# Norm steps, state space, head loads and paired scores moved in one two-layer kernel on a Trainium2 core

## The chip, the cores and the metric

The kernel runs on one core of one Trainium2 chip. A core has TensorE (PE in the profile, which multiplies and transposes), VectorE (DVE), ScalarE (ACT) and GpSimd (POOL), each with its own instructions in a fixed order, and SyncE (SP), whose queue issues nearly all loads and stores. Engines wait for each other only where a semaphore is named. The metric is the device time of one execution, in microseconds. The kernel before took 3650.94 us, the median of three runs (3649.84 to 3656.97).

## The reference

Two layers of a language model on 1024 tokens of width 1024, in float32. The first layer puts 16 more tokens ahead, so it works on 1040.

```python
# layer 1, mixer
h = rmsnorm(x, g_pre); u,q,k,v,o,gi,gf,ga,gb = split(h @ w_in)
y_a = gelu(s5_ssm(u, ...)); y_a = y_a * sigmoid(y_a @ w_glu)        # state space
hb  = mlstm_chunkwise(q, k, v, log_i, log_f)                        # gated matrix memory
merged = sigmoid(ga) * (y_a @ w_a) + sigmoid(gb) * (norm(hb) * sigmoid(o) @ w_b)
x = x + rmsnorm(merged @ w_out, g_post)
# layer 1, channel mixer
h = rmsnorm(x, g_pre)
x = x + rmsnorm((gelu(conv(h @ w_gate)) * (h @ w_up)) @ w_down, g_post)
# layer 2
proj = rmsnorm(x) @ w_in_2
y_rwkv = rwkv7_mixer(proj[..., :RWKV])     # 8 heads of 64, a recurrence over time
y_attn = dilated_attention(proj[..., RWKV:])   # 8 heads of 64, causal, three patterns in one softmax
x = x + concat(y_rwkv, y_attn) @ w_out_2
x = x + (silu(conv(rmsnorm(x) @ gate)) * (rmsnorm(x) @ val)) @ w_down_2
return rmsnorm(x)
```

A softmaxed score of the attention is q times k over the 64 numbers of one head.

## The kernel before

Activations lie with their 1024 features on 8 x 128 partitions and the tokens along the free axis. A product in float32 is made of three matmuls: each operand is split into a rounded part and a rest (hi and lo), and hi x hi, lo x hi and hi x lo are added up in one bank. `dense` does a tile of 128 output features: for each chunk of tokens (264, 264 and 512 in layer 1, 512 and 512 in layer 2) 8 x 3 matmuls into one bank. Weights are loaded by SP four tiles ahead and split two tiles ahead, hi by ACT and lo by DVE (`w_hi`, `w_lo`).

The order of every engine is written out by hand. A `Lane` stands for one engine. The stages follow one another: norm, first projections (in1: u, v, o, q, k and NG of the 16 g tiles), the state space's output gate (glu), the other g tiles (in2), the merge and w_out (out1), the channel mixer (ffn), the second layer's projections (in3), its heads, and again out and ffn. What runs beside a stage is a generator in `bg`, whose pieces end in `yield`. `tick` advances it by `rate` steps at the end of each chunk: RS = 3 beside in1 for the state space, RM = 4 beside in2 for the mLSTM, 1 beside glu for the gate transposes (`mgates`). With `fine` set, `slots(1)` after each three matmuls on PE, and `slots(8)` at each chunk on ACT and DVE, advance it by a step each; this is how norms are worked into the tiles of the next stage. PRE is the number of empty steps before the state space's first matmul, which wants `ssm_Cop`, made by POOL from DVE's `ssm_W`.

A joined norm (`joined_pe`, `joined_act`, `joined_dve`, `joined_pool`) ends a layer's part: a sum of squares over features by a matmul with ones (the root "sum"), then for eight row blocks m: DVE scales the block (`SCALAR_TENSOR_TENSOR HB<-HB,vecs,over1l..`), POOL adds the residual, ACT squares it, and DVE adds the square to the last ones; the root "sum2" by PE; then eight blocks y are scaled and split into hi and lo for the next stage. It is done for each half of the tokens: in the profile these are the tiles `extra` (first half) and `over1lB` and `over1lA` (second half). `plain_*` and `final_*` are norms with one root, in layer 2.

in3 has 52 tiles. Its results are stored to DRAM (`rkv`, `attn`), since the heads need the memory. The heads are three streams braided step by step: rwkv for two groups of heads, the second LAG = 20 steps behind, and attention. The attention for a pair of heads j goes over 16 units u, that is the row block i = u // 2 and the head h = u % 2; scores, mask and maximum by DVE, exponential by ACT, transposes by PE, copy by ACT, values by PE, copy by ACT. Its banks are a ring of four (`atb`), taken in turn: `take` waits until the old contents of a bank were read. The query is kept as `a_qz`, 128 partitions by two copies, with zeros in the other head's 64 rows, so that one 128-row matmul gives the score of one head.

## Time and profile before

| what | value |
|---|---|
| median of three runs | 3650.94 us |
| the profiled execution's own time | 3654.43 us |
| its span in the profile | 3652.6 us |
| TensorE busy | 3327.2 us, 91% |
| VectorE busy | 1757.6 us, 48% |
| ScalarE busy | 1187.3 us, 33% |
| GpSimd busy | 236.9 us, 6% |
| mean granted clock of TensorE | 0.954 |

A busy share is an average over stages that are limited by different things. Where TensorE is idle, the page and the trace name the engine and the tile whose semaphore released it; that name is inferred from the last event. A matmul of 128 rows by 512 columns comes every 0.22 us at the full clock. "PEclk" is the granted clock as a share of full speed: 0.50 is 1.2 GHz, 1.00 is 2.4 GHz.

### The profile page before, as it was taken

The page shows a single profiled execution, that of the slowest core. Times are in us where ns is not written, and L with a number is a line of the kernel's source. Part 1 is how long each engine was busy: PE and PEld are TensorE (multiplying, and loading weights), DVE is VectorE, ACT ScalarE, POOL GpSimd, SP SyncE. Part 2 cuts the span into 40 slices and gives each one's busy share as a digit, 9 for nine tenths or more (in the row PEclk, how much of TensorE's full clock was granted, in tenths as well). Part 3 has the DMA queues.
Part 4 walks back from the last instruction along what each step waited for, and adds up shares of the span by engine and source line. Part 5 has one row for each costly group of instructions (what it writes and reads, how often), then busy time and mean ns, then how long its engine had stood idle before and what let it go on. Part 6 is the DMA issues. An engine that isn't in the chain of part 4 may idle for free. (4 is left out here: it accounts for less than half of the span.)

```text
span 3652.6 us, 55140 instructions
## 1 busy us (share of the span) xinstructions
PE 3327.2 (91%) x23686; PEld 2767.0 (76%) x23686; DVE 1757.6 (48%) x2928; ACT 1187.3 (33%) x2054; POOL 236.9 (6%) x212
## 2 busy tenths in 40 slices
PE   5699989998979999999889978988977999999998
PEld 4588877787858888888667857776756778888887
DVE  6544533336475243435664435454554664333355
ACT  4112335542353221213433233434322432212133
POOL 1211000002130000000120000000001000000000
PEclk9899999999989999999999989998989999999999
DMA  2111112213423111123433330001001322111123
GB/s 98 41 53 47 65 62 84 80 55 125 142 75 120 59 46 53 42 61 109 135 135 128 130 108 19 10 28 36 2 19 39 107 89 71 49 47 52 47 93 110
DMA packets 86834, 262.28 MB, mean 72 GB/s; under 512 B 10272, under 2 KB 10400, under 8 KB 86464
## 3 DMA queue, kind: packets, MB, share of 16 engines
q1 hardware_dynamic: 76576, 224.07, 18.7%
q0 software_dynamic: 5120, 16.86, 1.3%
q10 hardware_dynamic: 4896, 17.84, 1.2%
q8 instruction: 187, 3.06, 0.4%
q14 instruction: 55, 0.45, 0.0%
HBM read 216.51 MB, written 42.21 MB: 71 GB/s over the span
## 5 line engine op out<-in xcount | busy, mean ns | idle before, releaser
L157 DVE TENSOR_TENSOR w_lo<-w_raw,w_hi 128x1024 fp32r<-128x1024 f32 (+3 forms) x353 | 398.3, 1130 | 440.5 <-ACT w_hi L154 438.4
L123 PE MATMUL ps<-XHA,w_hi 128*128 128x264 f32 (+3 forms) x1456 | 475.0, 326 | 20.6 <-DVE XLA L157 6.6
L123 PE MATMUL ps<-XLA,w_hi 128*128 128x264 f32 (+3 forms) x1456 | 462.9, 318 | 0.0
L123 PE MATMUL ps<-XHA,w_lo 128*128 128x264 f32 (+3 forms) x1456 | 461.2, 317 | 0.0
L154 ACT ACTIVATE w_hi<-w_raw 128x1024 fp32r<-128x1024 f32 (+3 forms) x353 | 339.9, 963 | 347.7 <-PE ps L123 285.0
L123 PE MATMUL ps<-XHB,w_hi 128*128 128x512 f32 x920 | 369.5, 402 | 9.2 <-POOL XLB L157 6.2
L123 PE MATMUL ps<-XLB,w_hi 128*128 128x512 f32 x920 | 360.6, 392 | 0.0
L123 PE MATMUL ps<-XHB,w_lo 128*128 128x512 f32 x920 | 360.2, 392 | 0.0
L123 PEld LDWEIGHTS ps<-XHA,w_hi 128*128 128x128 f32 x1456 | 281.6, 193 | 53.9 <-issue 25.0
L123 PEld LDWEIGHTS ps<-XLA,w_hi 128*128 128x128 f32 x1456 | 281.6, 193 | 22.6 <-issue 4.6
L123 PEld LDWEIGHTS ps<-XHA,w_lo 128*128 128x128 f32 x1456 | 281.7, 193 | 16.6
L123 PEld LDWEIGHTS ps<-XHB,w_hi 128*128 128x128 f32 x920 | 174.1, 189 | 52.4 <-issue 11.6
L123 PEld LDWEIGHTS ps<-XLB,w_hi 128*128 128x128 f32 x920 | 174.1, 189 | 38.2 <-issue 3.6
L123 PEld LDWEIGHTS ps<-XHB,w_lo 128*128 128x128 f32 x920 | 173.9, 189 | 37.0
L157 DVE TENSOR_TENSOR HB<-HB,ps 128x512 f32<-128x512 f32 (+1 forms) x136 | 88.4, 656 | 218.2 <-PE ps L123 215.7
L123 PE MATMUL ps<-X2HA,w_hi 128*128 128x512 f32 x416 | 163.6, 393 | 11.0 <-DVE X2LA L157 5.2
L123 PE MATMUL ps<-X2HB,w_hi 128*128 128x512 f32 x416 | 162.7, 391 | 1.4 <-issue 1.4
L123 PE MATMUL ps<-X2LA,w_hi 128*128 128x512 f32 x416 | 162.8, 391 | 0.0
L123 PE MATMUL ps<-X2HA,w_lo 128*128 128x512 f32 x416 | 162.7, 391 | 0.0
L123 PE MATMUL ps<-X2HB,w_lo 128*128 128x512 f32 x416 | 161.9, 389 | 0.0
L123 PE MATMUL ps<-X2LB,w_hi 128*128 128x512 f32 x416 | 161.8, 389 | 0.0
L164 DVE TENSOR_SCALAR C<-G,vecs 128x512 f32<-128x512 f32 x88 | 49.8, 566 | 224.7 <-ACT G L154 224.7
(446 smaller groups left out, 6344.1 us busy)
## 6 DMA issues: line engine op xcount, KB each, us to landing
w_raw<-in_f_gate SPq DMA_DIRECT2D x66, 512.0 KB, 3.3
w_raw<-in_f_up SPq DMA_DIRECT2D x66, 512.0 KB, 3.3
w_raw<-in_w_out SPq DMA_DIRECT2D x32, 512.0 KB, 3.4
w_raw<-in_f_down SPq DMA_DIRECT2D x48, 320.0 KB, 2.9
w_raw<-in_f_down SPq DMA_DIRECT2D x32, 384.0 KB, 3.1
w_raw<-in_w_rkv SPq DMA_DIRECT2D x24, 512.0 KB, 3.4
w_raw<-in_w_attn SPq DMA_DIRECT2D x24, 512.0 KB, 3.4
w_raw<-in_w_qkvo SPq DMA_DIRECT2D x16, 512.0 KB, 3.3
```

Of the source, the lines that this page charges most:

```text
L123: return Issued(e.matmul(out, a, b, start=start, stop=stop))
L154: return Issued(self.eng and self.eng.activation(out, src, ACT.Copy))
L157: return Issued(self.eng and self.eng.tensor_tensor(out, a, b, op))
L164: return Issued(self.eng.tensor_scalar(out, a, s1, s2, op0, op1))
```

## The change

Five things are changed together.

1. Two more g tiles go from in2 to in1 (NG 2 to 4), the state space begins 24 steps later (PRE 18 to 42), and the mLSTM runs at five steps per chunk (RM 4 to 5) beside the 12 g tiles that are left.
2. The gate transposes pause 10 steps where they paused 3, and are not drained after glu: they are done after the first chunk of in2.
3. Chunks up to 300 columns wide give a turn after every second k only (`turns_at`). The joined norm's pieces stand three turns apart (its blocks m) and two (its blocks y), and PE's roots later; the plain norms likewise.
4. Loads and constants of the heads are issued beside in3: at the tile `EARLY` the lora weights, the mask and the first rwkv inputs (`rwkv_load`), at `LATER` the first attention inputs (`attention_load`). The heads' memory is laid out anew, so that these land on tiles nobody uses then.
5. The query is one tile without zeros (`a_q`). The scores of two heads are two 64-row matmuls, on the upper and the lower half of the partitions, one behind the other in PE's order. PE's steps of a pair are now: transpose of the unit before, values of the one before that, scores of both.

Removed and added lines of the core:

```diff
-LAG, K0, RS, RM, NG, PRE, MID, POST, HN, Q1, Q2, Q3, Q4, Q5 = 20, 1, 3, 4, 2, 18, 18, 8, 8, 1, 1, 1, 1, 1
+LAG, K0, RS, RM, NG, PRE, MID, POST, HN, Q1, Q2, Q3, Q4, Q5 = 20, 1, 3, 5, 4, 42, 18, 8, 8, 1, 1, 1, 1, 1
...
-            if k < kt - 1:
+            if k < kt - 1 and turns_at(cn, k):
                 P.slots(1)
+def turns_at(cn, k):
+    return cn > 300 or k % 2
...
 def joined_pe(P, K, N, c):
-    yield from pause(4)
+    yield from pause(7)
     root_pe(P, K, N, c, "sum", ("acc", c, 7))
-    yield from pause(8)
-    yield from pause(8)
-    yield from pause(8)
+    yield from pause(37)
     root_pe(P, K, N, c, "sum2", ("acc2", c, 7))
-    yield from pause(16)
+    yield from pause(18)
...
 def joined_dve(V, K, N, c, gain, gnext, free):
-    yield from pause(8)
+    yield from pause(11)
     free(V)
     root_dve(V, N, c, "sum")
-    yield from pause(4)
...
         if m >= 2:
             add(m - 2)
-        yield
+        yield from pause(3)
+    yield
     add(6)
+    yield from pause(3)
     add(7)
-    yield from pause(12)
+    yield from pause(7)
     root_dve(V, N, c, "sum2")
...
+EARLY, LATER = (1, "rkv", 6), (1, "aqkv", 8)
...
+        if t == EARLY:
+            n3_over(D, K)
+            D.dma(K.wl[:, :], K.I["lora_wa"]).then_inc(K.lora, by=16)
+            D.dma(K.gl[:, :], K.I["lora_g"]).then_inc(K.lora, by=16)
+            D.dma(K.amask[:, :], K.I["a_mask"]).then_inc(K.a_mask, by=16)
+            for g in range(2):
+                ...
+                rwkv_load(D, K, g, 0)
+        if t == LATER:
+            ...
+            attention_load(D, K, 0)
...
+def rwkv_load(D, K, g, u):
+    T, (j, hf) = K.rw[g], halves(g)[u]
+    for n in range(3):
+        D.dma(T.in3[:, n, :], K.rkv[4 * n + j][:, 512 * hf:512 * hf + 512]).then_inc(T.ld, ("in", u), by=16)
...
+def attention_load(D, K, j):
+    S = K.at
+    D.dma(K.aq[:, :], K.attn[j]).then_inc(K.a_ld, by=16)
+    D.dma(K.ak[:, :], K.attn[4 + j]).then_inc(K.a_ld, by=16)
+    if j:
+        D.wait_ge(S.pe, ("t", j - 1, 15))
+    D.dma(K.aA[(18 * j) % 2][:, :], K.attn[8 + j]).then_inc(K.a_ld, ("in", j), by=16)
...
-                    P.mm(b[:, 0:cn], K.qz[:, h, 128 * i:128 * i + 128], K.ak[:, c0:c0 + cn], True, True).then_inc(
-                        S.pe, ("s", j, u, c0))
+        def scores(u):
+            i = u // 2
+            chunks = [(c0, min(512, 128 * (i + 1) - c0)) for c0 in range(0, 128 * (i + 1), 512)]
+            banks = [[ps.take(P, ("s", j, u + h, c0)) for c0, _ in chunks] for h in range(2)]
+            for n, (c0, cn) in enumerate(chunks):
+                for h in range(2):
+                    P.mm(banks[h][n][:, 0:cn], K.aq[heads(h), 128 * i:128 * i + 128], K.ak[heads(h), c0:c0 + cn], True,
+                         True).then_inc(S.pe, ("s", j, u + h, c0))
         for u in range(18):
+            if u % 2 and u < 16:
                 yield
             if 1 <= u < 17:
+                turn(u - 1)
             if u >= 2:
+                values(u - 2)
+            if u % 2 == 0 and u < 16:
+                scores(u)
+                yield
             yield
```

What moves, on PE in the first projections, where `ssm_Cop,ssm_Bn` is the state space's first matmul and the `XHA`, `XLA` rows are the projection's. Before:

```order
L123 MATMUL ps<-XHA,w_hi 128x264
L123 MATMUL ps<-XLA,w_hi 128x264
L123 MATMUL ps<-XHA,w_lo 128x264
L122 MATMUL ps<-ssm_Cop,ssm_Bn 32x256 x8
L123 MATMUL ps<-XHA,w_hi 128x264
L123 MATMUL ps<-XLA,w_hi 128x264
L123 MATMUL ps<-XHA,w_lo 128x264
```

It stands there after the first chunk of the fourth tile. Now:

```order
L123 MATMUL ps<-XHB,w_hi 128x512
L123 MATMUL ps<-XLB,w_hi 128x512
L123 MATMUL ps<-XHB,w_lo 128x512
L122 MATMUL ps<-ssm_Cop,ssm_Bn 32x256 x8
L123 MATMUL ps<-XHA,w_hi 128x264
L123 MATMUL ps<-XLA,w_hi 128x264
```

It moved behind the last chunk of a tile, eight chunks or 192 matmuls on.

On DVE in the first joined norm of a layer, beside the last tiles of w_out: `HB<-HB,vecs,over1lB` is the scaling of a block, `extra<-extra` and `extra<-extra,over1lB` the adds of squares, `over1lB<-over1lB,extra` and `w_lo` the tiles' own work. Before:

```order
L167 SCALAR_TENSOR_TENSOR HB<-HB,vecs,over1lB 128x514 x4
L157 TENSOR_TENSOR extra<-extra,over1lB 128x514
L157 TENSOR_TENSOR over1lB<-over1lB,extra 128x512
L157 TENSOR_TENSOR w_lo<-w_raw,w_hi 128x1024
L167 SCALAR_TENSOR_TENSOR HB<-HB,vecs,over1lB 128x514
L157 TENSOR_TENSOR extra<-extra 128x514
L167 SCALAR_TENSOR_TENSOR HB<-HB,vecs,over1lB 128x514
L157 TENSOR_TENSOR extra<-extra,over1lB 128x514
L167 SCALAR_TENSOR_TENSOR HB<-HB,vecs,over1lB 128x514
L157 TENSOR_TENSOR extra<-extra 128x514
```

Now:

```order
L167 SCALAR_TENSOR_TENSOR HB<-HB,vecs,over1lB 128x514 x2
L157 TENSOR_TENSOR over1lB<-over1lB,extra 128x512
L157 TENSOR_TENSOR w_lo<-w_raw,w_hi 128x1024
L167 SCALAR_TENSOR_TENSOR HB<-HB,vecs,over1lB 128x514 x2
L157 TENSOR_TENSOR extra<-extra,over1lB 128x514
L167 SCALAR_TENSOR_TENSOR HB<-HB,vecs,over1lB 128x514
L157 TENSOR_TENSOR extra<-extra 128x514
L157 TENSOR_TENSOR over1lB<-over1lB,extra 128x512
L157 TENSOR_TENSOR w_lo<-w_raw,w_hi 128x1024
L167 SCALAR_TENSOR_TENSOR HB<-HB,vecs,over1lB 128x514
```

The tiles' work now stands after every second or third block instead of once.

On PE in the heads, in the attention's fourth and fifth row blocks: `a_k,a_qz` or `a_k,a_q` are scores, `cst,a_A` transposes, `a_VT,a_PT` values, the others rwkv's. Before:

```order
L123 MATMUL ps<-a_k,a_qz 128x384
L123 MATMUL ps<-r_t,cst 128x512
L126 MATMUL ps<-cst,a_A 128x128 x3
L123 MATMUL ps<-a_VT,a_PT 128x64 x2
L123 MATMUL ps<-r_Xa,r_GB 64x64 x16
L123 MATMUL ps<-a_k,a_qz 128x512
```

Now:

```order
L126 MATMUL ps<-cst,a_A 128x128 x3
L123 MATMUL ps<-a_VT,a_PT 128x64 x2
L123 MATMUL ps<-r_Xa,r_GB 64x64 x16
L126 MATMUL ps<-cst,a_A 128x128 x3
L123 MATMUL ps<-a_VT,a_PT 128x64 x3
L123 MATMUL ps<-a_k,a_q 128x512 x2
```

Two scores stand together, behind two turns of transposes and values.

## Rows read from the trace of the kernel before

**Rows 1.** The page, part 1: busy us (share) xinstructions
```profile
PE 3327.2 (91%) x23686; PEld 2767.0 (76%) x23686; DVE 1757.6 (48%) x2928; ACT 1187.3 (33%) x2054; POOL 236.9 (6%) x212
```

**Rows 2.** Waits of PE: engine, tile, line, releaser: total us, times, longest
```profile
PE ps L123 <- DVE r_in L157: 31.1, 25, 3.6
PE ps L123 <- DVE extra L157: 26.0, 2, 14.4
PE ps L122 <- POOL ssm_Cop L163: 25.4, 1, 25.4
...
PE ps L123 <- DVE over1lB L157: 19.4, 2, 19.0
...
PE ps L123 <- DVE over1lA L157: 15.7, 1, 15.7
...
PE ps L126 <- ACT HB L136: 11.9, 1, 11.9
PE ps L123 <- DMA r_gl<-in_lora_g: 11.9, 1, 11.9
...
PE ps L126 <- DMA a_A<-attn: 6.9, 1, 6.9
```

**Rows 3.** Timeline, first projections: start, us, engine, line, operation, [idle <-releaser]
```profile
124.70 1.22 DVE L157 TENSOR_TENSOR w_lo<-w_raw,w_hi 128x1024 fp32r<-128x1024 f32 x1
124.88 7.28 POOL L163 TENSOR_SCALAR ssm_Cop<-ssm_W,cst 128x1152 f32<-128x1152 f32 x2 [8.93 <-DVE ssm_W L157]
...
132.21 1.93 PE L122 MATMUL ps<-ssm_Cop,ssm_Bn 128*32 128x256 f32 x16 [25.44 <-POOL ssm_Cop L163]
```

**Rows 4.** Timeline of ACT, output gate of the state space
```profile
524.62 1.07 ACT L136 ACTIVATE HB<-HB 4x1040 f32<-4x1040 f32 x1 [10.31 <-DVE HB L157]
...
527.00 0.88 ACT L136 ACTIVATE glu_s<-ps 128x264 f32<-128x264 f32 x2
```

**Rows 5.** Windows: us; busy PE, PEld, DVE, ACT, POOL; clock, DMA share, GB/s
```profile
545.00:845.00 300.00, 272.81 (x1617) 231.42 (x1616) 104.76 (x200) 150.43 (x257) 14.19 (x15) 0.95 0.21 74
1013.50:1016.00 2.50, 2.50 (x7) 1.95 (x6) 0.87 (x1) 2.42 (x5) 0.00 (x0) 0.50 0.23 39
2200.00:2650.00 450.00, 404.01 (x6240) 324.22 (x6239) 238.51 (x480) 163.62 (x372) 15.72 (x10) 0.93 0.06 19
```

**Rows 6.** Timeline of DVE, first norm of the group
```profile
989.56 4.62 DVE L167 SCALAR_TENSOR_TENSOR HB<-HB,vecs,over1lB 128x514 f32<-128x514 f32 x4
...
1011.25 0.70 DVE L157 TENSOR_TENSOR extra<-extra,over1lB 128x514 f32<-128x514 f32 x1
```

**Rows 7.** Timeline of DVE, second norm of the group
```profile
1068.61 0.74 DVE L167 SCALAR_TENSOR_TENSOR HB<-HB,vecs,over1lB 128x512 f32<-128x512 f32 x1
1069.45 1.78 DVE L157 TENSOR_TENSOR over1lB<-over1lB 128x512 f32<-128x512 f32 x1
```

**Rows 8.** Timeline of PE, second channel mixer
```profile
2940.26 0.47 PE L123 MATMUL ps<-X2HA,w_hi 128*128 128x512 f32 x1 [3.46 <-issue]
```

**Rows 9.** Timeline of all engines, start of the heads
```profile
2142.61 0.56 SPq L192 DMA_DIRECT2D r_wl<-in_lora_wa  x1
...
2151.09 0.69 DVE L157 TENSOR_TENSOR r_t<-r_t 128x512 f32<-128x512 f32 x1
...
2155.24 1.97 PE L126 MATMUL ps<-cst,a_A 128*128 128x128 f32 x8 [6.86 <-DMA a_A<-attn]
...
2157.43 1.92 PE L123 MATMUL ps<-r_t,cst 128*128 128x512 f32 x2
```

**Rows 10.** The tile a_qz on PE: duration ns min/median/max, first, last, forms
```profile
L123 PE MATMUL ps<-a_k,a_qz x192: 272/592/1220, 2157.0 to 2626.5; 128*128 128x512 f32 x96, 128*128 128x128 f32 x32, 128*128 128x256 f32 x32, 128*128 128x384 f32 x32
```

**Rows 11.** Timeline of PE and ACT in the heads
```profile
2192.33 1.13 PE L123 MATMUL ps<-r_WA,r_wl 32*128 32x512 f32 x4
...
2241.19 0.22 ACT L154 ACTIVATE HB<-ps 128x64 f32<-128x64 f32 x1
...
2309.57 2.04 PE L123 MATMUL ps<-r_WA,r_wl 32*128 32x512 f32 x4
```

224 lines of the change are left out of this document (117 added, 107 removed).

## The prediction

> **What bounds the kernel now.** The page's first part comes first: TensorE (PE) is busy 3327.2 of 3652.6 us and VectorE 1757.6 [rows 1], so the multiplies' own time is the floor and a change can win by closing PE's idle stretches or by making its instructions overlap. The list of waits by engine then names the idle ones [rows 2]: 25.4 us for one POOL result, 26.0, 19.4 and 15.7 us for four sums of norms made by VectorE, 11.9 us for an exponential of the gates, 11.9 and 6.9 us for two loads at the start of the heads. Each of these belongs to an edit of the change. The timelines around them [rows 3, 4, 6, 7, 9] say what the released work would do next; the windows and the score rows [rows 5, 10, 11] are for the two edits that change how densely PE is fed. The profiled execution took 3654.43 us, 1.8 beyond its span and 3.5 above the median of 3650.94; the sum is made against 3654.4, and 3.5 is taken off at the end. What this kernel's measurement can tell from no change is about 0.2%, 7.3 us.
>
> **1. State space 24 steps later.** PE stops inside the fourth projection tile and resumes 25.44 us later, at 132.21, because the state space's first matmul stands there in its order and wants Cop, which POOL finishes at 132.2 [rows 3]. VectorE's and POOL's preparation keep their places. With 24 steps at three per chunk the matmul stands eight chunks on, so tile four (begun at 101.9, 11.5 us of matmuls) ends near 113.6 and tile five near 125.1. Tile six's lo weights are split from 124.70 to 125.92, since VectorE waits for POOL's Bop before: 0.8 us is late next. Cop is ready long before PE gets to it. After the stall PE's 264-wide matmuls run 0.22 us apart instead of 0.12, at the lower of the two clocks (granted 0.50 where the same happens at 1013.5 [rows 5]), about 1.5 us. Sum: -25.4 - 1.5 + 0.8 = **-26** (-22 to -28). The two g tiles moved from the second to the first projection stage cost the same matmuls in either place: 0.
>
> **2. Gate transposes after the first chunk of the next stage.** They wait 11.88 us for the exponential, which itself waits for VectorE's scans and ends at 525.7 [rows 2, 4]. But the sigmoids of the output gate stand behind that exponential on ScalarE and start at 527.00 [rows 4], and PE has four banks to fill before it needs one of them. So PE stops a few chunks later for nearly as long: about 3 us go, and the 2 us of the first wait for m_D behind it: **-5** (-2 to -12, the whole wait).
>
> **3. The mLSTM five steps to a chunk instead of four.** Same steps beside 12 tiles, not 14. PE is idle 300.00 - 272.81 = 27.2 us in its stretch [rows 5], mostly on short chains of other engines of 0.7 to 3.1 us at a time. These chains' lengths stay, the cover shrinks to four fifths, so I let the idle grow by a quarter: **+7** (-3 to +27, the idle doubled).
>
> **4. Norms spread.** Four times PE reaches the second root sum before VectorE has it: 11.6, 19.0, 14.4 and 15.7 us (the extra and over1l rows [rows 2]). In PE's order that sum now stands 44 rows later (116 rows of 258 columns for the second), 10 us of matmuls (13.7). But VectorE's order now has the work of the tiles between the norm's steps, and that work delays the sum. For the first: first scaling at 989.56, last square added at 1012.0 [rows 6], 22.4 us of which 3.5 are idle. It starts 1.1 us later, and where one weight split and one add of the tiles' stood between the steps there are now four and five: 3 x 1.23 + 4 x 0.69 = 6.5 us more, and they take up the idle 3.5: 989.6 + 1.1 + 22.4 - 3.5 + 6.5 = 1016.1, against PE there at 1010.4: a stall of 5.7, 5.9 less. The same sum for the others, whose first scalings start at 1047.37, 1721.69 and 1825.33 and whose stalls begin at 1053.9, 1730.3 and 1834.9: 1047.4 + 3.4 + 25.4 - 3.9 + 5.1 = 1077.4 against 1067.6 (9.2 less); 1721.7 + 1.1 + 22.9 - 1.8 + 5.7 = 1749.6 against 1740.3 (5.1 less); 1825.3 + 1.1 + 25.2 - 3.5 + 5.4 = 1853.5 against 1844.9 (7.1 less). The last addend is two more splits and four or five of the tiles' other operations, 0.55 to 0.77 us each, counted in the two orders. Sum **-27**. Bounds: 0 if ScalarE's waits come in again at each step, -65 if all four vanish (60.7 and 1.2 each of low clock). The price per step carries this: VectorE needs 0.74 for a scaling and 1.78 for the add [rows 7], 2.5 together, while the last add, with POOL done, takes 0.70 [rows 6]. The adds are long beside POOL's residual add, which starts when the scaling ends, and spreading doesn't change that.
> The Trainium skill, "SBUF — State Buffer", in its summary of rules for kernel authors, says that when VectorE reads two operands from SBUF while GpSimd reads there, the later one waits for the other. The rows agree (1.78 against 0.70). By that rule a spread norm is still blocked for all of POOL's time if VectorE has tile work then, which is my sum; only where the spread leaves VectorE idle beside POOL would the adds fall to 0.70, which is rival A.
> Beside the last output projection and the second channel mixer the simple norms are spread too; PE's waits for it at 2892.11, 2940.26 (3.46 us [rows 8]) and 2947.7 are 6.5 us: **-5.5** (0 to -7).
>
> **5. Heads' loads made earlier.** PE has 11.9 us of idle until the lora weights' landing, then 6.9 until the attention's v [rows 2]: SP issues the first of them at 2142.61, after the last spill has landed, and v lands by 2155.24 [rows 9]. Now all but the last tiles' spills come ahead of them. What stays is the last projection's spill, so PE starts at about 2142.5, 3.8 earlier. After the scores its next matmul (at 2157.43) needs r_t, which VectorE has at 2151.8 [rows 9]; 3.8 earlier that is 2148.0, and v no longer stands before it, so 2157.4 - 2148.0 = 9.4 is gained: **-9.4** (-6 to -12). Twelve loads now go out among the weights' of the projection's last tiles; one that made a weight 4 us late would cost 4, and the lower bound leaves it in. POOL's memsets go from a time when nobody waits: 0.
>
> **6. Two heads' scores by row groups.** Now a score multiplies 128 rows, half of them zeros: 192 records [rows 10], 36,864 columns in all. After, two heads' scores stand in two halves of 64 rows, next to each other in PE's order. What rows show of such a pair: of the lora pairs (two row groups, 512 columns each), one at 2192.33 takes 1.13 us for both and one at 2309.57 2.04 us [rows 11]; in the first the two overlap, in the second a bank's wait stood between them. So a 512-wide pair is worth 0.91 us, and 36 of them (36,864 / 1024) 32.8 us of PE. Against it: from the fifth row block a pair takes all four banks and waits for ScalarE's copy of the values just computed (0.22 us [rows 11], 0.5 with the way there): 16 pairs, 8 us. PE is busy 404.01 of 450 us there [rows 5], the rest is waited for VectorE's chains, so I let 0.8 of 24.8 reach the span: **-20** (+5: they run one after the other, and the wait is paid; -35: all).
> The Trainium skill speaks on both sides: "TensorEngine Tiling (Array Packing)", key properties, lets different tiles load and multiply in parallel, and says that changing the tiling mode drains TensorE. The fast lora pair agrees with the first. No row here separates the second; the pairs need fewer such changes than single scores, not more, so it is no part of the sum.
>
> **Sum.** -26 - 5 + 7 - 27 - 5.5 - 9.4 - 20 = -85.9: 3654.4 - 85.9 = 3568.5, less 3.5 of the median: **3565**.
>
> **Rivals.**
> A, the norms' stalls vanish: VectorE is only 48% busy over the kernel and idles 3.5 us for ScalarE in the first of these norms, and such idle time would take the tiles' work. Against it the in-order sum above. 38 more: 3527.
> B, heads and mLSTM give less: row groups side by side need both weights in place and no bank wait between; the slow lora pair speaks for it, and the mLSTM's idle grows by 20 rather than 7. 20 + 13: 3598; with the norms giving only half, 3612.
> C, slower than before: the take of four banks ties the heads' three braided streams to each other. ScalarE's copies stand behind its waits for rwkv's steps, those behind PE's, and PE stands at the scores. VectorE's r_in is waited for 25 times already, up to 3.6 us each [rows 2]. The scores' 20 us would be gone and 16 waits of 0.5 us (8 in all, in the sum already) would be longer ones; the whole comes to 3658 and is slower from (3658 - 3565 - 20 + 8) / 16 = 5.1 us a wait on. At 6 us: 3565 + 20 - 8 + 96 = 3673. Against it, ScalarE's copy starts within 0.1 us of the values' end in the row at 2241.19 [rows 11].
> D, the scores run as before in time, and all else holds: 3565 + 20 + 5 = 3590; the pairs' records would not start together.
>
> **How the numbers follow.** Forecast 0.52, A 0.15, B 0.16, D 0.14, C 0.03. The likeliest is 3565, its own range 3545 to 3585. The range reaches to A and past D and B, without B's worst: 3525 to 3606. Faster by over 7.3 us holds A, B, D and the forecast but for their ends: 0.95; within it 0.02, from those ends; slower 0.03, C.
>
> **What would show it.** The profile after: no wait of PE for Cop, and the clock full from 102 on; the four waits for extra and over1l at 6, 10, 9 and 9 us (all gone: A; as before: step 4 is wrong); the waits for r_gl and v gone; PE's busy time 25 to 35 us less, the score records of two heads starting within 0.01 us of each other and their mean near today's; the stretch of in2 with about 34 us idle. The prediction is wrong if the sum2 waits keep their length, if the heads' stretch (671 us from 2147 to 2818) is not shorter by 15, or if a new wait for ScalarE's HB stands before the scores.

## The result, and the profile after

The changed kernel takes 3630.81 us, the median of four runs (3630.16 to 3631.42), beside 3652.1 for the kernel before in its four runs of the comparison: a ratio of 0.994 (95%: 0.9923 to 0.9957). It is faster, by 21 us, and not by the 86 that were forecast; 3565 and the range up to 3606 were both missed. The profiled execution took 3631.2 us with a span of 3629.4, 23.2 less than the 3652.6 before.

Part 1 of the page after, which answers to [rows 1]:

```profile
PE 3319.5 (91%) x23686; PEld 2772.5 (76%) x23686; DVE 1741.7 (48%) x2928; ACT 1181.3 (33%) x2050; POOL 242.1 (7%) x210
```

PE has as many matmuls as before and is busy 7.7 us less, where 25 to 35 were forecast. The place of the difference is found by cutting both spans at the same matmuls. The two g tiles (22.8 us) that went from in2 to in1 are taken out of both.

| stretch | before | after | change, without the moved tiles | forecast |
|---|---|---|---|---|
| first projections | 455.72 | 456.80 | -21.7 | -26 |
| output gate | 39.33 | 37.17 | -2.2 | -5 |
| in2 beside the mLSTM | 291.03 | 284.42 | +16.2 | +7 |
| merge to first w_down, first pair of joined norms | 366.16 | 358.84 | -7.3 | -15.1 |
| around the second pair | 235.91 | 229.67 | -6.2 | -12.2 |
| heads, from in3's last matmul to w_out's first | 687.46 | 687.96 | +0.5 | -29.4 |
| w_out and start of the second channel mixer | 230.11 | 228.09 | -2.0 | -5.5 |

The rest (1,347 us) differs by 0.4. Nearly half of what is missing lies in one row, the heads.

The waits of PE after (engine, tile, line, releaser: total us, times, longest), the answer to [rows 2]:

```profile
PE ps L123 <- DVE r_in L157: 37.9, 27, 3.6
...
PE ps L123 <- DVE m_SS L167: 21.1, 13, 3.8
...
PE ps L123 <- DVE r_t L157: 20.2, 21, 3.9
PE ps L123 <- DVE r_S L157: 18.6, 27, 3.8
PE ps L123 <- DVE extra L157: 13.7, 2, 9.0
PE ps L123 <- ACT r_BK L154: 13.5, 5, 4.1
PE ps L123 <- DVE ssm_Dop L177: 13.1, 3, 7.8
...
PE ps L123 <- ACT glu_s L136: 12.1, 1, 12.1
PE ps L123 <- DVE over1lB L157: 8.9, 1, 8.9
PE ps L123 <- DVE over1lA L157: 8.0, 1, 8.0
...
PE ps L123 <- ACT HB L154: 6.8, 17, 0.6
```

Gone are the rows for POOL's Cop, for the two loads at the start of the heads, and for the exponential. The norms' rows fell from 61.1 to 30.6 us. But four kinds are new or longer: the gates' sigmoid `glu_s` (12.1, in the place of the exponential's 11.9), `m_SS` of the mLSTM (8.2 before), rwkv's four tiles `r_in`, `r_t`, `r_S` and `r_BK` (31.1, 13.9, 13.4 and 9.1 before), and 17 short ones for `HB`, the copy of the attention's values.

The timeline of PE and DVE at the places of steps 1, 2 and 4 (start, us, engine, line, operation, [idle before <- releaser]):

```profile
124.38 2.35 DVE L157 TENSOR_TENSOR w_lo<-w_raw,w_hi 128x1024 fp32r<-128x1024 f32 x2
...
528.25 0.79 PE L123 MATMUL ps<-glu_h,w_hi 128*128 128x512 f32 x1 [12.06 <-ACT glu_s L136]
...
1008.30 2.08 PE L123 MATMUL ps<-extra,cst 128*128 128x258 f32 x4 [4.72 <-DVE extra L157]
...
1028.22 0.36 PE L123 MATMUL ps<-XHA,w_hi 128*128 128x258 f32 x1 [1.15 <-POOL XLA L157]
...
1073.80 2.07 PE L123 MATMUL ps<-over1lB,cst 128*128 128x512 f32 x2 [8.93 <-DVE over1lB L157]
...
1103.74 0.36 PE L123 MATMUL ps<-XHA,w_hi 128*128 128x258 f32 x1 [2.22 <-issue]
...
1724.66 0.47 PE L123 MATMUL ps<-XHB,w_hi 128*128 128x512 f32 x1 [2.16 <-issue]
...
1737.36 2.07 PE L123 MATMUL ps<-extra,cst 128*128 128x512 f32 x2 [9.01 <-DVE extra L157]
...
1772.74 0.50 PE L123 MATMUL ps<-PH1B,w_hi 128*128 128x512 f32 x1 [3.16 <-DVE PL1B L157]
...
1840.59 2.07 PE L123 MATMUL ps<-over1lA,cst 128*128 128x512 f32 x2 [8.04 <-DVE over1lA L157]
```

Each norm still has its root wait (4.7, 8.9, 9.0, 8.0), and beside it stand waits that were not there: the first matmuls on the blocks that the spread norm has just made, and two at 1103.74 and 1724.66 for which the profile names no releaser. PE stops at 528.25 for the sigmoids as long as it stopped for the exponential.

The start of the heads and a pair of scores on PE, for [rows 9] and [rows 11], and the tile of the scores, for [rows 10] (durations in ns, lowest/median/highest):

```profile
2121.26 2.07 PE L123 MATMUL ps<-r_WA,r_wl 32*128 32x512 f32 x4 [8.33 <-issue]
...
2126.51 2.04 PE L123 MATMUL ps<-r_t,cst 128*128 128x512 f32 x2 [0.55 <-DVE r_t L157]
...
2280.41 1.13 PE L123 MATMUL ps<-a_k,a_q 64*128 64x512 f32 x4
```

```profile
L123 PE MATMUL ps<-a_k,a_q x192: 269/589/1218, 2125.2 to 2601.4; 64*128 64x512 f32 x96, 64*128 64x128 f32 x32, 64*128 64x256 f32 x32, 64*128 64x384 f32 x32
```

Both parts of the change to the heads do what they say. From in3's end to the matmul of `r_t` it is 14.4 us where it was 23.9. One pair of scores of 512 columns takes 1.13 us for both, the records of the two start 7 ns apart (35 ns in the second chunk of a wide row block), and PE is occupied by scores 42.8 us in all where it was 82.6 (the union of the 192 records). And yet the stretch is as long as before. Where the 39.8 us went, the windows of that stretch tell (us; busy PE, PEld, DVE, ACT, POOL with counts; mean granted clock, DMA share, GB/s). Before:

```profile
2133.58:2821.04 687.46, 568.54 (x9154) 453.21 (x9154) 345.72 (x670) 225.24 (x486) 28.75 (x21) 0.90 0.08 23
```

After:

```profile
2112.07:2800.03 687.96, 551.56 (x9154) 453.55 (x9154) 341.93 (x669) 224.99 (x484) 25.97 (x17) 0.87 0.05 18
```

PE is busy 17 us less, not 40, its clock fell from 0.90 to 0.87, and it is idle 136.4 us instead of 118.9. To put a price on the clock, each stretch below is cut into windows of 2 us, and PE's busy time in each is parted into busy x granted clock ("work", what it would take at 2.4 GHz) and the rest ("lost to the clock", what the same matmuls took longer at 1.2 GHz). Stretch = work + lost + idle. Each row is one execution, the profiled one. All kernels are in the table, since the experiments are read by it.

| heads of | stretch | work | lost to the clock | idle |
|---|---|---|---|---|
| before | 687.5 | 519.7 | 48.8 | 118.9 |
| after | 688.0 | 484.2 | 67.3 | 136.4 |
| e1 single scores, old order | 684.5 | 522.0 | 57.4 | 105.1 |
| e2 new order, full rows | 701.0 | 512.9 | 58.1 | 130.0 |
| e3 rate by chunk | 687.8 | 484.2 | 66.9 | 136.7 |
| e4 blocks y closer | 676.0 | 485.7 | 54.3 | 136.0 |
| e5 gates spread | 688.0 | 484.3 | 67.2 | 136.5 |
| e6 pairs inside the old order | 677.4 | 509.9 | 56.5 | 111.0 |
| e7 eight idle matmuls ahead | 681.1 | 492.0 | 58.8 | 130.2 |
| e8 root later, y closer | 676.0 | 485.8 | 54.3 | 136.0 |
| e9 all together | 675.9 | 517.1 | 52.9 | 105.9 |
| e10 after + 40 idle of 256 columns | 684.3 | 508.8 | 55.3 | 120.2 |
| e11 e9 with the norms of after | 677.3 | 516.5 | 55.8 | 105.0 |
| e12 e1 + eight idle matmuls ahead | 687.8 | 529.4 | 56.2 | 102.3 |
| e13 after + 40 idle of 512 columns | 698.0 | 526.3 | 53.8 | 117.9 |
| e14 e9 + 40 idle of 256 columns | 689.5 | 540.6 | 56.4 | 92.5 |
| e15 before + 40 idle of 256 columns | 690.5 | 542.8 | 39.2 | 108.5 |

From before to after the work fell by 35.5 us; 17.5 of it came back as idle time and 18.5 as time lost to the lower clock. The two are not equally firm. after, e3, e4, e5 and e8 have the same instructions in the heads: their work and idle times agree to 1.6 and 0.7 us, while 66.9 to 67.3 us are lost to the clock in three of them and 54.3 in the other two.

### The profile page after: what moved, and what is told of

Same layout as the page of the kernel before. It is cut to its first block, busy times and chain, and to the rows that moved or that the text cites. A ratio compares the mean times of both kernels' runs of the same rounds, so it can differ in the third digit from the quotient of the medians.

```text
span 3629.4 us, 55150 instructions
## 1 busy us (share of the span) xinstructions
PE 3319.5 (91%) x23686; PEld 2772.5 (76%) x23686; DVE 1741.7 (48%) x2928; ACT 1181.3 (33%) x2050; POOL 242.1 (7%) x210
## 4 chain that ended last, share of the span: by engine, by line
PE 76%; DVE 14%; ACT 6%; issue 3%; DMA 1%; POOL 1%; ACTq 0%; DVEq 0%; SPq 0%; POOLq 0%
PE ps L123 73%; PE ps L122 2%; PE ps L126 2%; DVE w_lo L157 1%; ACT L136 1%; ACT w_hi L154 1%; DVE r_t L157 1%; DVE HB L167 1%; DVE m_S L167 1%; DVE r_in L157 1%; ACT m_D L136 1%; DVE HB L157 1%; DVE r_Xa L157 1%; DVE r_t L167 0%; ACT r_t L136 0%
```

## The experiments

Each ratio is against the kernel before on the same chip. "Idle matmuls" are matmuls whose result nobody reads.

Most kernels here share all stages but one with after, so the traces also tell how far a stage moves when nothing in it is changed:

| stretch | kernels with after's instructions there | us |
|---|---|---|
| first projections | all but before and e15 | 454.7 to 456.9 |
| output gate | all of those but e5, e9, e11, e14 | 37.2 to 38.4 |
| in2 | after, e1, e2, e4, e6, e7, e8, e10, e12, e13 | 282.5 to 287.9 |
| merge to first w_down | all but before, e15, e4, e8, e9, e14 | 355.7 to 358.9 |
| around the second pair | the same | 229.4 to 229.7 |
| heads | after, e3, e4, e5, e8 | 676.0 to 688.0 |
| w_out and start of the channel mixer | all but before, e15, e4, e8 | 226.4 to 228.1 |

A difference inside such a range is not shown to be the edit's.

### Which part of the change to the scores costs what

The first kernel gives each score its own step again, in the old order, but with 64 rows:

```diff
-            if u % 2 == 0 and u < 16:
-                scores(u)
-                yield
...
+            if u < 16:
...
+                    b = ps.take(P, ("s", j, u, c0))
+                    P.mm(b[:, 0:cn], K.aq[heads(h), 128 * i:128 * i + 128], K.ak[heads(h), c0:c0 + cn], True, True).then_inc(
```

> The changed kernel with the attention's PE and ScalarE steps in their order of before: each head's scores alone, in their own step, as 64-row matmuls on the unpadded query. The early loads and all else stay. Read is the heads' stretch, from the end of the last projection matmul to the first matmul of the output projection: 687.5 us before, 688.0 us in the changed kernel. Theory one (the order of pairs costs what their overlap gives): the stretch falls to 678, the early loads' 9 us being the only gain left, and the kernel runs at 3621 instead of 3631. Theory two (the early loads gain nothing, since another chain is as late as they were): 687, and 3630. TensorE's busy time of the score records goes back from 43 us to about 80 in both.

The second keeps the pairs' order and lets both matmuls use all 128 rows, so that they cannot run side by side (each score is then the sum over both heads, not what the reference computes):

```diff
-                    P.mm(banks[h][n][:, 0:cn], K.aq[heads(h), 128 * i:128 * i + 128], K.ak[heads(h), c0:c0 + cn], True,
+                    P.mm(banks[h][n][:, 0:cn], K.aq[:, 128 * i:128 * i + 128], K.ak[:, c0:c0 + cn], True,
```

> The changed kernel with its order of pairs, but each score multiplies all 128 rows (query and key of both heads), so that the two of a pair can't overlap: the scores are those of the two heads added up, which is not what the reference computes. TensorE gets about 40 us of matmuls back, in the same places. Theory one (TensorE's time counts in the heads, and the pairs' order costs about as much): the stretch grows from 688 by 20 to 35 us, to 708 to 723. Theory two (the heads are bound by chains over VectorE and ScalarE, and time taken from TensorE turns into its waiting): it grows by less than 8, to at most 696, and TensorE's waits for r_in, r_t and r_S shrink by about 30 us.

Measured: e1 3627.27 us (0.9935, 0.9921 to 0.995), e2 3645.63 (0.9989, 0.998 to 0.9999). Windows of the heads, e1:

```profile
2111.67:2796.22 684.55, 579.40 (x9154) 457.68 (x9154) 346.04 (x669) 223.62 (x484) 25.88 (x17) 0.89 0.05 18
```

and e2:

```profile
2107.05:2808.09 701.04, 571.01 (x9155) 461.14 (x9154) 342.70 (x669) 225.08 (x484) 25.98 (x17) 0.89 0.05 17
```

Both stretches lie between the two theories of their kernel: 684.5 between 678 and 687, 701.0 between 696 and 708. e2's profiled execution is the fastest of its ten, 3638.38 us, so its 701.0 is rather short than typical.

The three kernels part the edit in two. The order alone (e1 to e2) adds 24.9 us of idle time and makes the stretch 16.5 longer. It takes 9.1 us of work away: two scores that stand one behind the other overlap in part, and the records of all scores occupy PE 73.1 us in e2 and 84.6 in e1. Full rows or half rows make no difference to a single score (median record 592 and 589 ns). Running side by side (e2 to after) takes 28.7 us of work away, of which 13 reach the end: 6.4 return as idle and 9.2 to the clock. So in work and idle time together the order costs 15.8 us and the overlap gains 22.3, and the pairs of after are 6.5 us ahead of e1. That the stretch of after is 3.4 us longer than e1's all the same is 9.9 us more lost to the clock, and this part is not the edit's for certain: e4 and e8 have the same pairs and take 676.0. The waits of PE in the heads show where the order costs. e1:

```profile
PE ps L123 <- DVE r_in L157: 29.5, 25, 3.6
...
PE ps L123 <- DVE r_t L157: 14.3, 16, 3.6
PE ps L123 <- DVE r_S L157: 13.3, 20, 3.8
PE ps L123 <- ACT r_BK L154: 9.1, 4, 4.1
```

e2:

```profile
PE ps L123 <- DVE r_in L157: 33.2, 26, 3.6
PE ps L123 <- DVE r_t L157: 18.7, 21, 3.8
PE ps L123 <- DVE r_S L157: 18.0, 26, 3.8
PE ps L123 <- ACT r_BK L154: 13.6, 5, 4.1
...
PE ps L123 <- ACT HB L154: 6.9, 17, 0.6
```

The banks (`HB`, 6.9) are the smaller part and are what the prediction had priced at 8. The larger are rwkv's own chains, 17.3 us longer over four rows. In the old order each of the braid's steps had some attention work, which covered a chain. With pairs, by the `yield`s of the new code, two of every four steps have none.

The sixth kernel puts that to use: the old order, and a pair only for the first four row blocks, where it needs two banks:

```diff
+                both = (0, 1) if i < 4 else (h,)
+                if h in both[0:1]:
+                    for c0 in range(0, 128 * (i + 1), 512):
+                        bs = [ps.take(P, ("s", j, 2 * i + g, c0)) for g in both]
+                        for g, b in zip(both, bs):
+                            P.mm(b[:, 0:cn], K.aq[heads(g), 128 * i:128 * i + 128], K.ak[heads(g), c0:c0 + cn], True,
...
```

> The changed kernel with the attention in its order of before, each turn of transposes and values in the step after a score, but with the scores of both heads side by side, as two row groups, in the first four row blocks, where a pair needs two of the four banks; row blocks five to eight have single scores. 10 of 36 parts of the columns are paired. Read is the heads' stretch: 687.5 before, 688.0 in the changed kernel, 684.6 with single scores in the old order, 701.0 with the new order and no overlap. Theory one (the order of pairs leaves two of four steps without attention work, which costs about 16 us, and overlap is worth 13 to 25 for all columns): 677 to 682. Theory two (overlap gains nothing here since TensorE waits anyway): 684 to 686. If the early loads and single scores were already at the bound of VectorE's chains, theory two.

3617.51 us (0.9901, 0.9884 to 0.9917), 13.3 below after. The stretch is 677.4, inside the first theory's 677 to 682: idle stays near e1's (111.0) and 12 us of work are gone. So it is better than e1. Against after it proves less. Work and idle time together are 620.9 us in e6 and 620.6 in after, and the 10.6 us between the stretches are all clock; e4 and e8, with every score in a pair and the order of after, are at 676.0. Which of the two orders is the better one in the heads stays open.

### The lower clock in the heads

One pair of kernels was not made for this and says the most. e4 (below) and after have the same instructions in the heads. Their first 40 us, after:

```profile
2121.26:2161.26 40.00, 33.38 (x276) 23.64 (x276) 17.70 (x36) 18.32 (x46) 2.94 (x2) 0.60 0.00 1
```

and e4:

```profile
2118.00:2158.00 40.00, 32.66 (x318) 22.73 (x320) 18.93 (x41) 19.73 (x48) 2.94 (x2) 0.75 0.01 1
```

The granted clock is 0.60 in the one and 0.75 in the other, and 276 against 318 matmuls are through. Over the whole stretch the same instructions take 688.0 and 676.0 us, with work and idle time equal to 1.5 us and 13.0 less lost to the clock. In both PE stood idle for the 8.3 us ahead of the first of these matmuls. It is not chance from one kernel to the next: the lower clock sets in 5.8 to 6.1 us ahead of the first matmul of the heads and lasts 37.5 us in after, e3 and e5, and it sets in 4.1 us ahead and lasts 20.5 in e4 and e8. It doesn't go by the time at which the heads begin either: in3 ends at 2108.8 in e4 and e8 and at 2100.4, 2107.2 and 2112.1 in e3, e5 and after.

Can matmuls that nobody needs buy the clock back? First, eight of them ahead of the heads, in the time of that wait:

```diff
 def heads_pe(P, K):
+    b = K.fg.take(P, "warm")
+    for _ in range(8):
+        P.mm(b[:, 0:512], K.ident, K.cst[:, 0:512], True, True)
```

> The changed kernel with eight matmuls of a 128x128 by 128x512 constant into a free bank put on TensorE between the last projection and the heads, where it is idle for 9.2 us. They compute nothing that is used. In the changed kernel the granted clock is 0.50 in the first 32 us of the heads; two executions with the same instructions in the heads took 678.8 and 666.9 us there, with 173 and 145 us at the lower clock. Theory one (the idle stretch ahead is what leaves the clock low, and the clock costs): less than 16 of the first 32 us are at 0.50, and the heads' 678.8 us fall by 4 to 12. Theory two (the start is a chain of ScalarE and VectorE and the clock falls again at once): within 3 us, and 2 us more where the matmuls last longer than the idle time.

3622.24 us (0.9917, 0.9902 to 0.9931): 681.1 instead of 688.0, and 8.5 us less lost. Less was lost here. The same eight put into e1:

> Single 64-row scores in the old order (its heads' stretch was 684.6, 3 us less than before, where the early loads should give 9.4) with the eight idle matmuls ahead of the heads. Theory one (the early loads' other 6 us were lost to the clock, which was at 0.50 for 31.6 us of the first 40 where it was 24.3 before): 677 to 680, and at most 25 us of the first 40 at the lower clock. Theory two (another chain is late there, whatever the clock): 683 to 686.

3629.45 us (0.9943, 0.9928 to 0.9958), 2 above e1 instead of below it, though the two intervals overlap. The stretch of 687.8 is longer than either theory had it. Its first 40 us:

```profile
2120.50:2160.50 40.00, 33.69 (x221) 22.53 (x222) 16.23 (x32) 16.27 (x41) 2.95 (x2) 0.56 0.00 1
```

The clock is 0.56 there, and 0.60 in e1 without the matmuls ahead. What they did is to put the fall off: the lower clock sets in 0.8 us behind the first matmul of the heads in e7 and 0.9 behind it in e12, where it came 5.8 and 5.9 ahead of it in after and e1. But it comes all the same, for 23.9 of the next 27 us in e7 and 41.0 of the next 44 in e12. My explanation, that the idle time ahead of the heads brings the clock down and filling it keeps it up, is not borne out; e7's 7 us are of the size of what e4 got by no edit of the heads.

Then 40 idle matmuls in the middle of rwkv's steps, each ahead of a wait for VectorE:

```diff
+            b = D.ps.take(P, (("Y", lv), u))
+            P.mm(b[:, 0:256], K.ident, K.cst[:, 0:256], True, True)
-            products(("Y", lv), lambda h, c: [(x.GB[heads(h), c, 0, :], x.X[heads(h), block(c)])])
+            products(("Y", lv), lambda h, c: [(x.GB[heads(h), c, 0, :], x.X[heads(h), block(c)])], b)
```

> The changed kernel with one more matmul on TensorE ahead of each wait of rwkv for the next power (40 times in the heads, a constant of 128x128 by 256 columns, about 0.43 us each, 17 us in all, into the bank that is overwritten next; nothing of it is used). The heads' stretch is 688.0 us with 173 us of it at the lower clock. Theory one (idle time of TensorE lowers its clock and that is why time taken from it doesn't reach the end): at most 160 us at the lower clock, and the stretch between 680 and 692 in spite of 17 us more work. Theory two (TensorE's time counts by itself, and the clock has little to do with it): 696 to 705, with the time at the lower clock within 10 us of 173.

3626.0 us (0.9934, 0.9917 to 0.995), with a stretch of 684.3: 24.6 us more work, 16.2 less idle, 12.0 less lost. With 512 columns instead of 256:

> The changed kernel with the 40 idle matmuls of 512 columns instead of 256, 34 us of added work for TensorE at the full clock instead of 17. Without them the heads' stretch was 688.0 us with 173 us at the lower clock, with the smaller ones 684.3 and 146. Theory one (the clock pays for added work up to a point, then TensorE's time counts): 125 to 145 us at the lower clock and a stretch of 686 to 698, longer than with 17 us of work but by less than the added 17. Theory two (the 3.7 us gained with the smaller ones were chance in where the clock fell): 700 to 710.

3639.07 us (0.9972, 0.9961 to 0.9983), stretch 698.0, the long end of the first theory: 42.1 more work against 18.5 of idle and 13.5 of the clock. In the kernel before, with 256 columns:

> The kernel before with the same 40 idle matmuls of 256 columns. Its heads' stretch is 687.5 us with 132 us at the lower clock, so the clock has less to give back, while there is more of TensorE's own work (scores 40 us longer). Theory one (the price of added work depends on how much of the stretch is at the lower clock): it grows by 2 to 12 us, clearly more than in the changed kernel, where 17 us of work took 3.7 away. Theory two (added work ahead of these waits is free in any case, since the waits are longer than it): within 2 of 687.5.

3651.92 us (1.0007, 0.9997 to 1.0016), stretch 690.5, 3.0 longer: 23.1 more work, 10.4 less idle, 9.6 less lost, as the first theory had it. So most of such work is paid for by idle time and clock that it takes away, but not all; only in after, the kernel with most idle time and most low clock, is the sum a gain. It is 4 us, work and idle time together are 8.4 us more, and the 12.0 of the clock are less than the 13.0 that e4 had without any edit of the heads; so this gain is not shown to be the idle matmuls'.

### The mLSTM's rate

Chunks of in2 are 264, 264 and 512 columns wide, and each gets five steps. Here they get 4, 4 and 7, the same 15 for a tile:

```diff
-LAG, K0, RS, RM, NG, PRE, MID, POST, HN, Q1, Q2, Q3, Q4, Q5 = 20, 1, 3, 5, 4, 42, 18, 8, 8, 1, 1, 1, 1, 1
+LAG, K0, RS, RM, NG, PRE, MID, POST, HN, Q1, Q2, Q3, Q4, Q5 = 20, 1, 3, (4, 4, 7), 4, 42, 18, 8, 8, 1, 1, 1, 1, 1
-    def tick(self):
-        self.step(self.rate)
+    def tick(self, c=0):
+        self.step(self.rate[c] if isinstance(self.rate, tuple) else self.rate)
```

> The changed kernel with the mLSTM's 15 steps to a tile dealt out 4, 4 and 7 to the chunks of 264, 264 and 512 columns instead of 5, 5 and 5. Read is the stretch from the end of the output gate's projection to the merge: 291.0 before with 14 tiles, 284.4 in the changed kernel with 12 (two tiles are 22.8 us, so 16.2 more than its matmuls). Theory one (the short chunks are too short to cover five steps): 284.4 falls by 5 to 10. Theory two (it is the density over the whole stage that is short, not its unevenness): within 3 of 284.4, since the wide chunk then carries seven steps with waits of their own.

3618.89 us (0.9914, 0.9899 to 0.9928), 11.9 below after. Windows of in2, before:

```profile
539.94:830.97 291.03, 266.63 (x1584) 226.26 (x1585) 93.25 (x194) 142.86 (x237) 1.66 (x8) 0.96 0.22 77
```

after:

```profile
538.60:823.02 284.42, 245.78 (x1458) 205.66 (x1459) 90.23 (x192) 131.43 (x227) 1.66 (x8) 0.96 0.20 72
```

and with 4, 4 and 7:

```profile
538.99:813.82 274.83, 240.65 (x1459) 201.47 (x1459) 90.28 (x192) 131.62 (x227) 1.67 (x8) 0.97 0.21 74
```

Idle time is 24.4, 38.6 and 34.2 us. The stretch with even dealing is 274.8 = 291.0 - 22.8 + 6.6: the 7 forecast for a denser mLSTM is what it costs if the steps are dealt by width. Of the other 9.6, 4.5 are idle time, from five steps beside a 264-wide chunk, whose matmuls are too short to cover them: in2 idles 37.2 to 40.0 us in the ten kernels with five steps and 33.2 to 34.2 in the four with 4, 4 and 7 (e3, e9, e11, e14). The other 5.1 are in the busy time of the same matmuls, at 0.96 of the clock instead of 0.97; 7.3 to 13.5 us are lost to the clock in the ten and 4.9 to 7.8 in the four, so how much of this is the dealing's is not settled.

### The joined norms

Blocks y are made one turn apart instead of two, so that the next stage's matmuls find them:

```diff
 def normed_dve(V, K, N, c, gnext, name):
-        yield from pause(2)
+        yield
...
     rest(7)
+    yield from pause(8)
```

> The changed kernel with the last part of each norm (the eight blocks y) one turn apart again, as before, the blocks m still three apart. Read are the stretches around the norms: from the merge's end to the first down projection 263.0 before and 255.4 in the changed kernel, and around the second norm pair 235.9 and 229.7. Theory one (the waits that came up anew, about 6 us at 1028 to 1040, 4 us at 1098 to 1108 and 7 us at 1724 to 1773 in the changed kernel, are for the y blocks that now come two turns apart): they go, and the stretches fall by 6 to 10 and by 3 to 7; in all 3618 instead of 3631. Theory two (they come from the second root standing 15 turns later): within 2 of the changed kernel.

3622.67 us (0.9925, 0.991 to 0.994), 8 below after. But the heads, in which nothing is changed, are 12.0 us shorter for their clock (above), and the span only 10.3 (3619.1 beside 3629.4), so the rest is longer by 1.7. By places: -1.5 around the first pair and -0.2 around the second, both inside the ranges of kernels without this edit, and +4.5 behind w_out of the second layer, far outside (232.6). That is the second theory's case. PE's timeline has other waits in the place of those that went:

```profile
1056.08 0.77 PE L123 MATMUL ps<-XHA,w_hi 128*128 128x512 f32 x1 [3.20 <-DVE w_lo L157]
...
1068.75 2.07 PE L123 MATMUL ps<-over1lB,cst 128*128 128x512 f32 x2 [7.51 <-DVE over1lB L157]
...
1761.01 0.77 PE L123 MATMUL ps<-XHB,w_hi 128*128 128x512 f32 x1 [5.15 <-issue]
...
2912.32 0.77 PE L123 MATMUL ps<-X2HA,w_hi 128*128 128x512 f32 x1 [5.05 <-issue]
```

The one at 1056.08 waits for a tile's weights: VectorE makes the blocks in a row and splits the weights behind them. For the last two the profile names no releaser. Next, e4 with the second root eight turns later on every engine:

```diff
 def joined_pe(P, K, N, c):
-    yield from pause(37)
+    yield from pause(45)
     root_pe(P, K, N, c, "sum2", ("acc2", c, 7))
-    yield from pause(18)
+    yield from pause(10)
```

> The kernel with the y blocks one turn apart (3622.7 us) and in it the second root of each joined norm eight turns, 5.5 us of matmuls, later on all engines, so that the norm ends where the changed kernel's does. Its four waits for that root are 4.7, 7.5, 9.0 and 8.0 us. Theory one (the sum arrives when VectorE's order lets it, and TensorE only gets there too early): each wait falls by about 4 to 5.5 us, 18 in all, and if nothing behind waits for the y blocks the kernel takes 3605. Theory two (the next stage then waits for the y blocks instead): the waits fall, but new ones of 3 to 6 us come at the next stage's first tiles, and it takes 3615 to 3623.

3620.68 us (0.991, 0.9896 to 0.9925). Of PE's waits for the root sums 0.9 us is left. It waits here instead:

```profile
1024.31 0.36 PE L123 MATMUL ps<-XHA,w_hi 128*128 128x258 f32 x1 [3.65 <-DVE XLA L157]
...
1069.41 0.49 PE L123 MATMUL ps<-XHA,w_hi 128*128 128x258 f32 x1 [2.78 <-DVE w_lo L157]
...
1103.70 0.55 PE L123 MATMUL ps<-XHA,w_hi 128*128 128x258 f32 x1 [7.14 <-DVE w_lo L157]
...
1766.64 0.76 PE L123 MATMUL ps<-PH1B,w_hi 128*128 128x512 f32 x1 [3.92 <-ACT w_hi L154]
```

The stretches around the pairs are 253.5 and 226.5 against 255.4 and 229.7 in after. Of the 29.7 us by which the root waits fell, 5 were won at most, which is the second theory's case: the 3.2 around the second pair are clear, the 1.9 around the first lie inside the range of kernels with after's norms (merge to first w_down is 356.9 here, and 355.7 to 358.9 there).

### The gate transposes

VectorE's scans of the gates are put into five steps instead of three, so that the output gate's multiplies stand between them, and the exponential comes three steps later on ScalarE:

```diff
     V.scan(g.a, g.c, g.b, 0.0, MUL, ADD).then_inc(d)
+    yield
...
     V.scan(g.m, g.negM, g.u, 0.0, ADD, MAX).then_inc(d)
+    yield
...
+    yield from pause(3)
     A.wait_ge(S.dve, "Bm")
```

> The changed kernel with the gates' work beside the output gate dealt out more thinly: VectorE's two scans and what follows them take five steps instead of three, and ScalarE's exponential comes three steps later. Read is the output gate's stretch, 39.3 us before and 37.2 in the changed kernel, with one wait of TensorE of 11.9 and 12.1 us. Theory one (the sigmoids wait because VectorE's multiplies stand behind some 10 us of scans in one lump): the wait falls to under 5 us and the stretch to 28 to 31. Theory two (only the exponential ahead of the sigmoids on ScalarE counts, 1.07 us and a table load of 1.28): 2 to 3 us go.

3626.35 us (0.9927, 0.9912 to 0.9941), and the output gate's stretch is 33.1 us against 37.2. Its wait:

```profile
528.52 0.80 PE L123 MATMUL ps<-glu_h,w_hi 128*128 128x512 f32 x1 [6.38 <-ACT glu_s L136]
```

So the 12 us in after were ScalarE's queue: the sigmoids behind an exponential that waits for scans. Half of it went, more than the second theory allowed and less than the first asked for.

### All together

e9 has the rate of e3, the gates of e5, the pairs of e6, the eight matmuls of e7 and the joined norms of e8, with the plain norms of after. e11 is the same with the joined norms of after, e14 is e9 with 40 idle matmuls.

> The changed kernel with all that gained alone: the mLSTM's steps dealt 4, 4 and 7 (about 9.5 us), the gates' work spread (4.5), the attention in its old order with pairs in the first four row blocks (10.6), eight idle matmuls ahead of the heads (7, in part the same low clock as the pairs'), and in the joined norms the second root eight turns later and y one turn apart (5, the other norms as in the changed kernel). Theory one (the stages are separate and the gains add): 3630.8 - 9.5 - 4.5 - 10.6 - 4 - 5 = 3597. Theory two (a stage's time hangs on the clock that the one ahead left, so they don't add): 3603 to 3612.

> The same but with the joined norms exactly as in the changed kernel. Theory one (the later root and the faster y gain 2 us around the first norm pair, 3 around the second): 5 us more than the kernel with all. Theory two (they only move the wait to the next stage): within 2 us of it.

> The kernel with everything that gained alone (3597.4 us, heads' stretch 675.9 with 142 us at the lower clock) and the 40 idle matmuls of 256 columns. Theory one: as in the kernel before, the clock has less to give back than in the changed kernel, and the stretch is 676 to 686. Theory two (idle matmuls gain wherever waits are): 668 to 674, and the fastest kernel of all, at 3592.

| kernel | median us | ratio (95%) |
|---|---|---|
| e9 | 3597.42 (3595.61 to 3598.84) | 0.9856 (0.9841 to 0.987) |
| e11 | 3601.38 | 0.9868 (0.9854 to 0.9883) |
| e14 | 3615.48 (3602.92 to 3617.52) | 0.9902 (0.9884 to 0.9919) |

The gains add up to the 3597 that were forecast, with some luck in the parts: the heads gave 12.1 us where 14.6 were summed, and the stages ahead of the merge 16.9 where it was 14. e9 is the fastest kernel here, 33 us below after and 53 below before. Its heads (675.9) are no shorter than those of e4 and e8, which have none of its edits there. The norms' share is 4 us by the medians, with intervals that overlap, and 1.4 of it lies in the heads. The idle matmuls cost it 18, 13.6 of them in the heads, whose 689.5 are above what the first theory allowed: 23.5 us more work, 13.4 less idle, and 3.5 more lost to the clock. One of e14's four runs took 3602.92 us at a mean granted clock of 0.963, the others over 3614.5 at 0.959 to 0.961; why its clock was higher is open.

## Why the prediction was wrong

The sign held, and most mechanisms are in the profile as described. Of the 62.7 us between the sum and the span, 29.9 are steps 5 and 6 (6.5 of it step 5 and 23.4 step 6, parted at e1), 13.5 the joined norms, 9.2 the mLSTM, 4.3 the state space, 3.5 the plain norms and 2.8 the gates; the rest of the kernel gave 0.4.

**Step 1, right.** PE does not stop for Cop, and -26 came out at -21.7 in this profile (-21.6 to -23.9 over the kernels that have the edit). The clock is 1.00 from 105 to 132, three us later than forecast. The lo weights of tile six were split at 124.38, as forecast. Some of the rest is the wait for `ssm_Dop`, 5.5 us before and 13.1 now: a chain with its first matmul moved meets its next operand.

**Step 2, mechanism right, size too high.** The sum took 3 us of the transposes' own wait and 2 of another as gone. PE's wait is 12.06 now where it was 11.88, and 2.2 were won. e5 shows what has to move: VectorE's scans, which hold the exponential, which holds the sigmoids.

**Step 3, right for a case that was not built.** "The cover shrinks to four fifths" treats chunks as alike. With steps by width it is +6.6, with five to each chunk +16.2 in after and +14.3 to +19.7 in the other kernels with this in2.

**Step 4, stalls right, their sum wrong.** Forecast root stalls of 5.7, 9.8, 9.3 and 8.6 were 4.7, 8.9, 9.0 and 8.0, and rival A, that they vanish, was given rightly little. But of 27 forecast only 13.5 were won. Of the 30.5 us by which the root waits fell, 10 came back as other waits of PE, 5.6 were lost to the clock and 1.3 are work. The step took a root wait for the only wait of a norm and had no term for the clock. PE then comes sooner to the next stage, and there the norm's blocks are late, or weights whose splits stand behind the norm's work in VectorE's order (the profile of e8 names them at the place of 1103.74): 1.15 at 1028.22, 2.22 at 1103.74, 2.16 at 1724.66 and 3.16 at 1772.74. For the 2.16 at 1724.66, ahead of the root, no profile names the releaser. e8 shows that waits move: with these root waits gone the two stretches shrink by 5 us at most.

**Step 5, right where it was read, and then eaten.** The matmul of `r_t` comes 9.4 us sooner after in3's end, as forecast. In e1, which has this edit with the old order, the stretch is 2.9 shorter and not 9.4: 13.8 less idle against 8.6 more lost to the clock and 2.3 of work. The step had no term for the clock.

**Step 6, the step that failed.** The forecast saw 32.8 us of PE saved; it was 39.8 of records and 28.7 of work between e2 and after. Of these 28.7, 22.3 are left when the idle time that came for them is taken off, 0.78, which is the share of 0.8 that was forecast, and the banks cost 6.8 where 8 were. The error was in the two terms that the sum put at nothing. The first is the order: the edit is two edits, and the pairs' order thins the cover of rwkv's chains. It adds 24.9 us of idle time, the banks' among them, and takes 9.1 of work (e1 to e2). The second is the clock, 9.9 us more lost than in e1. So from e1 to after the step gave -22.3 + 15.8 + 9.9 = +3.4 us where -20 was forecast. "0.8 of 24.8" was taken from how busy PE is in the stretch as it was, which says nothing of an order not yet there. Without the clock's part the step still gave 6.5 and not 20. Rival C had the right place (three braided streams tied to each other) and the wrong cause, ScalarE behind the banks; D, that the overlap fails, is refuted by the 7 ns. The Trainium skill, "TensorEngine Tiling (Array Packing)", key properties, says that different tiles load and multiply in parallel, and this trace agrees: 1.13 us for a pair, 1.12 for a single score of e1.

**What stays open.** Why the same heads run at 0.60 of the clock in their first 40 us in one kernel and at 0.75 in another, and lose 67.3 or 54.3 us over the stretch. The kernels differ only in what came before: e4 and e8 have the blocks y of the norms one turn apart, after, e3 and e5 two. Eight matmuls ahead went with 7 us less once and 3 more another time. With a step of 12 us that no edit of the heads chose, the gains of after, e1, e6, e7, e9 and e10 in the heads are not known to better than that; the order's 24.9 us of idle time and the overlap's 28.7 of work are, since idle and work agree to 1.6 us between after, e3, e4, e5 and e8.

## What to carry to other kernels

- Where a kernel feeds PE by steps dealt beside chunks, deal them by the chunk's width; and when two matmuls are put together to run at once, look which steps lose their filler: here the order took back 15.8 us of the 22.3 that the overlap gave.
- Removing a wait from an engine with a fixed order is worth its length less what is late next there. For a norm that is the blocks and weights of the next stage, and they are found by asking of each queue what was pushed back.
- In a sparsely fed stretch split the time into work, idle and lost to the clock before judging an edit. Less work and more idle can leave the span where it was. Before a few us are put down to an edit, look how far the stretch moves between kernels that have the same instructions in it.

## What the runs showed of the hardware

- Two 64-row matmuls of 512 columns in float32 on different halves of the rows take 1.13 us together, and one alone takes 1.12 (e1); the records of the two start 7 ns apart.
- The same instructions took 688.0 us in three kernels and 676.0 in two, with 67 and 54 us lost to the lower clock. Over all kernels the heads lost 39.2 to 67.3 us to it.
- 40 idle matmuls of 256 columns (23 to 25 us of work) moved the heads by -3.7 us in after, +3.0 in before and +13.6 in e9: filling idle time is no dependable cure for the clock.
